# Two layers of a hybrid diffusion backbone on one core: the step of the bidirectional scan reordered, its first products and copies moved ahead of the attention branch

## What is computed

```python
proj = h @ w_in                      # q k v | z | xBC | dt | u gv | gates, 1024 x 6928
y_att = attend(q, k, v)
y_ssm = ssm_branch(z, xbc, dt, ...)  # bidirectional scan, 8 heads x 64, state 64
y_gm  = gmlp_branch(u, gv, ...)
merged = g0 * (y_att @ w_branch[0]) + g1 * (y_ssm @ w_branch[1]) + g2 * (y_gm @ w_branch[2])
return merged @ w_o, ...
```

```python
acs    = cumsum(dt * a)
decay  = exp(where(lower, acs[i] - acs[j], -inf))
scores = einsum('bcihn,bcjhn->bcijh', cc, bc) * decay          # C.B products times the decay
y_diag = einsum('bcijh,bcjhp->bcihp', scores, x * dt)
y_off  = einsum('bcihn,bchpn,bcih->bcihp', cc, h_in, exp(acs)) # C times exp(acs), times the initial state
y      = y_diag + y_off (+ the flipped direction) + x * d_skip
y      = rms_norm(y * silu(z), norm_g)
```

## Time and profile before

| | before |
|---|---|
| median of 3 runs | 1352.4 us |
| profiled execution, its own time | 1351.62 us |
| its span | 1349.8 us |
| mean granted TensorE clock | 0.960 |
| TensorE busy | 1252.7 us, 93% |
| weight loads of TensorE busy | 977.7 us, 72% |
| VectorE busy | 1006.4 us, 75% |
| ScalarE busy | 741.4 us, 55% |
| GpSimd busy | 67.1 us, 5% |
| moved by DMA | 353.68 MB, 262 GB/s |

### The profile page before, as it was taken

How to read it: one execution, slowest core, us unless ns; L and a number is a source line. 1 busy time by engine, 2 the same in 40 slices (tenths; PEclk the granted TensorE clock), 3 DMA queues, 4 the chain that set the end, 5 groups by cost and what they waited for, 6 DMA issues and landing times.

```text
span 1349.8 us, 16800 instructions
## 1 busy us (share of the span) xinstructions
PE 1252.7 (93%) x6097; PEld 977.7 (72%) x6097; DVE 1006.4 (75%) x1154; ACT 741.4 (55%) x704; POOL 67.1 (5%) x113
## 2 busy tenths in 40 slices
PE   5999999989899999999989999998987999999994
PEld 1767777777676787877767777786776768788773
DVE  0646557787688888888877466678857988888886
ACT  1543454652655667677653454356345666666773
POOL 1400001001000000000020000010000000000000
PEclk8899898999989999999989989998998999999998
DMA  9978654537778999899976767353435798989991
GB/s 357 306 276 313 232 182 148 180 118 302 264 255 311 338 329 342 317 341 340 354 224 211 265 253 258 130 187 133 165 139 200 287 352 325 328 318 338 348 355 60
DMA packets 98092, 353.68 MB, mean 262 GB/s; under 512 B 9060, under 2 KB 12608, under 8 KB 81616
## 3 DMA queue, kind: packets, MB, share of 16 engines
q1 hardware_dynamic: 87504, 295.12, 61.0%
q0 software_dynamic: 10496, 57.39, 12.1%
HBM read 349.77 MB, written 3.74 MB: 262 GB/s over the span
## 4 chain that ended last, share of the span: by engine, by line
PE 60%; DVE 24%; ACT 4%; DMA 4%; issue 3%; DVEq 3%; ACTq 1%; SPq 1%; POOL 0%; POOLq 0%
PE bank L910 57%; DVE wl L1785 13%; PE bank L913 3%; ACT wh L1684 1%; DMA first<-in_w_ada 1%; DVE tmp L1785 1%; ACT wh L1477 1%; DMA adaw<-in_w_ada 1%; DVE merged L1785 1%; DVE hid L2475 1%; DMA decay<-decay_rows 1%; DVE x L1785 1%; ACTq L1572 1%; DMA raw<-in_moe_w 1%; ACT gate L1571 0%
## 5 line engine op out<-in xcount | busy, mean ns | idle before, releaser
L1785 DVE TENSOR_TENSOR wl<-raw,wh 128x2048 fp32r<-128x2048 f32 (+1 forms) x268 | 610.5, 2278 | 125.8 <-ACT wh L1477 77.6
L1684 ACT ACTIVATE wh<-raw 128x2048 fp32r<-128x2048 f32 x192 | 367.5, 1917 | 61.9 <-PE bank L910 47.7
L910 PE MATMUL bank<-wh,xgh 128*128 128x512 f32 x512 | 212.2, 414 | 5.2 <-DVEq L2444 5.1
L910 PE MATMUL bank<-wh,xgl 128*128 128x512 f32 x512 | 204.9, 400 | 0.0
L910 PE MATMUL bank<-wl,xgh 128*128 128x512 f32 x512 | 204.5, 399 | 0.0
L1477 ACT ACTIVATE wh<-raw 128x2048 fp32r<-128x2048 f32 (+1 forms) x76 | 142.3, 1872 | 103.9 <-PE bank L910 62.1
L910 PE MATMUL bank<-wh,hTh 128*128 128x512 f32 x448 | 188.0, 420 | 5.6 <-DVE wl L1785 3.4
L910 PE MATMUL bank<-wl,hTh 128*128 128x512 f32 x448 | 183.1, 409 | 0.0
L910 PE MATMUL bank<-wh,hTl 128*128 128x512 f32 x448 | 182.5, 407 | 0.0
L910 PEld LDWEIGHTS bank<-wh,xgh 128*128 128x128 f32 x512 | 98.3, 192 | 25.3 <-DVE xgl L1785 5.4
L910 PEld LDWEIGHTS bank<-wh,xgl 128*128 128x128 f32 x512 | 97.7, 191 | 23.8
(11 more groups left out here) (302 smaller groups left out, 1556.9 us busy)
## 6 DMA issues: line engine op xcount, KB each, us to landing
raw<-in_moe_w SPq DMA_DIRECT2D x256, 512.0 KB, 4.9
raw<-in_moe_w SPq DMA_DIRECT2D x64, 1024.0 KB, 5.2
raw<-in_w_in SPq DMA_DIRECT2D x52, 1024.0 KB, 6.1
adaw<-in_w_ada POOLq DMA_DIRECT2D x32, 1024.0 KB, 7.0
raw<-in_w_branch SPq DMA_DIRECT2D x12, 1024.0 KB, 5.2
raw<-in_w_ada SPq DMA_DIRECT2D x8, 1024.0 KB, 9.8
raw<-in_w_o SPq DMA_DIRECT2D x8, 1024.0 KB, 4.7
first<-in_w_ada SPq DMA_DIRECT2D x4, 1024.0 KB, 16.7
```

The source lines that it names most:

```text
L910: return behind(nc.tensor.matmul(*args, **kw))
L1684: tally(A_(wh[c][:, :], raw[:, r, :], ACT.Copy), part_high[c])
L1785: return V.tensor_tensor(o, a, b, op)
```

## The change

Six things are done, in both layers:

1. On TensorE the products `cb00`, `cb01` go ahead of the last gate fill of branch 0, `xs0`, `cb10`, `cb11`, `xs1` behind it and ahead of the attention branch, `bt` behind that branch. Before, all of them stood behind the cumulative sums. The plan of the banks follows.
2. On ScalarE the two copies of `xs` stand between the last gate copy and the root of the gv norm.
3. On VectorE the copies `cb_of(0)`, `cb_of(1)` and the one to `btok` stand around the gv norm and the two conversions, ahead of `merge(0)`; before, behind `sumrow`.
4. `eb` holds only the rows that are used, for two steps: `[P, 2, 2, P]`. The exponential is two instructions of 64 partitions x 256 instead of one of 128 x 512. It waits for the reader of the step two before and not of the step before.
5. The two products to `ctS` move from behind the subtraction to the end of the step, behind the conversion, and the subtraction no longer waits for `eb`.
6. The product of x and the skip factor is a function of its own, `skipped`. For the context it runs in step 1 into the upper half of `tmp`, for the latent tokens ahead of `branch_turned(2)`.

```diff
@@ -207,13 +207,11 @@
     odd("adaT2")
     sides(4, 5, 6, 7)
     turned(0)
+    odd("cb00"), odd("cb01"), odd("xs0"), odd("cb10"), odd("cb11"), odd("xs1")
     branch(0)
+    odd("bt")
     odd("sp0"), odd("sp1")
     odd("ac"), odd("acT")
-    for s in range(2):
-        odd(f"cb{s}0"), odd(f"cb{s}1")
-        odd(f"xs{s}")
-    odd("bt")
     odd("st0"), odd("st1")
     for n in range(8):
         if n % 4 == 3:
@@ -445,7 +443,7 @@
             ("S", [P, 4, 2 * P], F32, 6),
             ("pT", [P, 2, 4, P], F32, 10),
             ("yTh", [P, BC, 2 * P], F32R, 0), ("yTl", [P, BC, 2 * P], F32R, 4),
-            ("W", [P, 2, 4, P], F32, 0), ("eb", [P, 4, P], F32, 4),
+            ("W", [P, 2, 4, P], F32, 0), ("eb", [P, 2, 2, P], F32, 4),
             ("ctS", [P, 2, 2, P], F32, 6),
             ("decay0", [P, 4, P], F32, 8),
             ("cbm", [P, 2, 2, P], F32, 10),
@@ -1158,8 +1156,30 @@
                 fill(("gate", 0, 1, 0))
                 turn_mod(l, 2, "adaT2")
                 branch_rows(l, 0, q)
+                pe.wait_ge(xbc_ready, 3 * l + 3)
+
+                def state_products(s):
+                    for g in range(2):
+                        t = bank_free(pe, l, f"cb{s}{g}")
+                        r = slice(g * HD, (g + 1) * HD)
+                        ins = mm(t[:, 0:P], xbc[r, 4, s * P:(s + 1) * P], xbc[r, 5, s * P:(s + 1) * P], start=True, stop=True)
+                        fills(ins, f"cb{s}{g}")
+
+                def turn_state(s):
+                    turn4(l, f"xs{s}", [xbc[:, m, s * P:(s + 1) * P] for m in range(4)])
+
+                state_products(0)
                 fill(("gate", 0, 1, 1))
+                turn_state(0)
+                state_products(1)
+                turn_state(1)
                 branch(l, 0)
+                t = bank_free(pe, l, "bt")
+                turn(t[:, 0:P], xbc[:, 4, 0:P], ident)
+                for g in range(2):
+                    ins = mm(t[g * HD:(g + 1) * HD, P:2 * P], ident[:, (1 - g) * HD:(2 - g) * HD], xbc[:, 5, P:2 * P],
+                             start=True, stop=True)
+                fills(ins, "bt")

@@ -1183,20 +1203,6 @@
-                pe.wait_ge(xbc_ready, 3 * l + 3)
...
                 fill(GATES[2][0])
                 pe.wait_ge(bt_ready, l + 1)
                 for r in range(2):
@@ -1628,6 +1634,8 @@
                 branch_turned(0)
                 ahead(("gate", 0, 1, 1))
                 gate_take(0, 1)
+                for s in range(2):
+                    take(f"xs{s}", xs[:, s, :], ACT.Copy, xs_ready)
                 square_root(0)
                 ahead(("branch", 0, 0))
                 ahead(("branch", 0, 1))
@@ -1635,8 +1643,6 @@
 
                 act.wait_ge(rem_ready, l + 1)
                 A_(acs[:, 0, 16:32], acs[:, 0, 16:32], ACT.Exp).then_inc(rem_exp, 1)
-                for s in range(2):
-                    take(f"xs{s}", xs[:, s, :], ACT.Copy, xs_ready)
                 ahead(GATES[2][0])
                 for r in range(2):
                     if r == 0:
@@ -1647,9 +1653,11 @@
                 for n in range(8):
                     if n >= 4:
                         act.wait_ge(decay_in[n % 2], 16 * (4 * l + n // 2 + 1))
-                        if n >= 5:
-                            act.wait_ge(ct_done, 4 * l + n - 4)
-                        A_(eb[:, :, :], decay[n % 2][:, :, :], ACT.Exp)
+                        if n >= 6:
+                            act.wait_ge(ct_done, 4 * l + n - 5)
+                        for r in range(2):
+                            gp = slice(r * HD, (r + 1) * HD)
+                            A_(eb[gp, n % 2], decay[n % 2][gp, r:4:2, :], ACT.Exp)
                         act.drain().then_inc(eb_exp, 1)
                     act.wait_ge(seg_in, 8 * l + n + 1)
                     A_(seg[:, n % 2], seg[:, n % 2], ACT.Exp)
@@ -2191,12 +2199,23 @@
                     filled(3 * i + 2)
                 ahead(("gate", 0, 1, 0))
                 modulation(l, 2, "adaT2")
+                cbraw = ropet[:, :].rearrange("p (s g t) -> p s g t", s=2, g=2)
+                def cb_of(s):
+                    for g in range(2):
+                        t = bank_full(dve, l, f"cb{s}{g}")
+                        frees(V.tensor_copy(cbraw[:, s, g, :], t[:, 0:P]), f"cb{s}{g}")
+
                 branch_turned(0)
+                cb_of(0)
                 ahead(("gate", 0, 1, 1))
                 gv_norm()
+                cb_of(1)
                 early = dve.mark_branch_hint_location()
                 ahead(("branch", 0, 0))
                 ahead(("branch", 0, 1))
+                t = bank_full(dve, l, "bt")
+                frees(V.tensor_copy(btok[:, :], t[:, 0:2 * P]), "bt")
+                drain().then_inc(bt_ready, 1)
                 merge(0)
 
 
@@ -2220,17 +2239,6 @@
                 frees(V.tensor_copy(sumrow[:, :], t[0:32, 0:2 * P]), "acT")
                 drain().then_inc(sums_rows, 1)
 
...
                 ahead(GATES[2][0])
 
                 dve.wait_ge(rem_exp, l + 1)
@@ -2241,22 +2249,23 @@
                     tt(xw[:, r, :].rearrange("t (h d) -> t h d", h=HEADS), xs[:, 0, :].rearrange("t (h d) -> t h d", h=HEADS),
                        bc(wend[:, 8 * r:8 * r + 8], 2, HD), ALU.mult)
                     drain().then_inc(xw_ready, 1)
-                def scanned(s):
+                def skipped(s, y):
+                    tt(y.rearrange("t (h d) -> t h d", h=HEADS), xs[:, s, :].rearrange("t (h d) -> t h d", h=HEADS),
+                       bc(hrow[:, 32:40], 2, HD), ALU.mult)
+                    drain()
+
+                def scanned(s, y, squares):
 
                     if s == 0:
                         dve.wait_ge(z_ready, 2 * l + 2)
-                    y = tmp[:, 0:NW]
-                    tt(y.rearrange("t (h d) -> t h d", h=HEADS), xs[:, s, :].rearrange("t (h d) -> t h d", h=HEADS),
-                       bc(hrow[:, 32:40], 2, HD), ALU.mult)
-                    drain()
                     t = bank_full(dve, l, f"y{s}")
                     frees(tt(y, t[:, :], y, ALU.add), f"y{s}")
                     drain()
                     tt(z[:, s, :], y, z[:, s, :], ALU.mult)
                     drain()
-                    tt(tmp[:, NW:D], z[:, s, :], z[:, s, :], ALU.mult)
-                    drain()
-                    V.tensor_reduce(small[:, s:s + 1], tmp[:, NW:D], X, ALU.add)
+                    tt(squares, z[:, s, :], z[:, s, :], ALU.mult)
+                    drain()
+                    V.tensor_reduce(small[:, s:s + 1], squares, X, ALU.add)
                     drain()
 
                 for n in range(9):
@@ -2265,21 +2274,12 @@
                         if n in (0, 1):
 
                             bank_full(dve, l, f"st{n}")
-                        if n >= 4:
-                            dve.wait_ge(eb_exp, 4 * l + n - 3)
                         dve.wait_ge(decay_in[n % 2], 16 * (4 * l + n // 2 + 1))
                         for i in range(4):
                             h, r = 2 * j + i // 2, i % 2
                             V.tensor_scalar(seg[:, n % 2, i, :], decay[n % 2][:, i, :],
                                                   acs[:, s, 8 * r + h:8 * r + h + 1], 0.0, ALU.subtract, ALU.min)
                         drain().then_inc(seg_in, 1)
-                        if n >= 4:
-                            dve.wait_ge(y_sem, 8 * l + n - 1)
-                            for r in range(2):
-                                gp = slice(r * HD, (r + 1) * HD)
-                                state_out = xbc[gp, 5, P:2 * P] if r == j // 2 else btok[gp, P:2 * P]
-                                ins = tt(ctS[gp, n % 2], eb[gp, r:4:2, :], bc(state_out, 1, 2), ALU.mult)
-                            ins.then_inc(ct_done, 1)
                     if n >= 1:
                         m = n - 1
                         s, j = m // 4, m % 4
@@ -2300,10 +2300,21 @@
                         drain().then_inc(W_ready, 1)
                     if 1 <= n < 8:
                         ahead(SCAN_FILL[n - 1])
+                    if 4 <= n < 8:
+                        dve.wait_ge(eb_exp, 4 * l + n - 3)
+                        dve.wait_ge(y_sem, 8 * l + n - 1)
+                        for r in range(2):
+                            gp = slice(r * HD, (r + 1) * HD)
+                            state_out = xbc[gp, 5, P:2 * P] if r == n % 4 // 2 else btok[gp, P:2 * P]
+                            ins = tt(ctS[gp, n % 2], eb[gp, n % 2], bc(state_out, 1, 2), ALU.mult)
+                        ins.then_inc(ct_done, 1)
+                    if n == 1:
+                        skipped(0, tmp[:, NW:D])
                     if n == 6:
-                        scanned(0)
+                        scanned(0, tmp[:, NW:D], tmp[:, 0:NW])
+                skipped(1, tmp[:, 0:NW])
                 branch_turned(2)
-                scanned(1)
+                scanned(1, tmp[:, 0:NW], tmp[:, NW:D])
```

27 lines of the change are left out of this document (2 added, 25 removed).

## The result

The changed kernel took 1354.65 us (median of 10 runs, 1350.47 to 1356.87), the kernel before beside it 1350.55 (median of 10, among them the three shown above). The ratio of the runs is 1.0026, 95% interval 1.0014 to 1.0038: under the 2% that counts as a change, but 3.5 us and clear of noise. The difference of the two medians is 4.1 us. I had forecast no difference. The profiled execution took 1355.28 us, its span is 1353.5 against 1349.8.

The account below looks back on a forecast made before the run. The chain ended last on TensorE for 60% of the span, but a VectorE-ScalarE loop bounded the changed stretch. Terms 2 x 0.1 + 2 x 0.0 + 0.5 - 0.7 gave 0.0 us, so 1352.4 us; range 1347.5 to 1358.

Parts of the forecast that it names:

- Front, ScalarE: Root of the gv norm: 0.45 us of passes and 1.4 of x copies ahead make it 1.85 late.
- Front, VectorE: Copies moved ahead of the row sums add 1.1 us; with the late root, their copy starts 2.95 later.
- the clock risk: Rival, chance 0.03: clock stays down after TensorE's 3.5 us wait before the states; some 2 us a layer, 1356.4.
- Front, TensorE: Next gate fill ends 5.3 us earlier; not kept, as state products wait 3.5 us for xw, running from 228.3.
- Start of the scan: First subtraction in layer 0: first decay tile lands last, at 230.65; scan starts at 230.7, 0.6 us earlier.
- an upper bound: Third step's start: +0.4 us if a 1 MB weight load competes with decay tiles or the clock falls.
- To sub 2: Third step's start, with the early skip product of 0.69 + 0.08: +0.1 us, between -0.6 and +0.4.
- Steps 4 to 7: Scan with ctS at step ends and eb's wait gone: -1.45, +0.5, +0.1, +0.87, together 0.0 us a layer.
- the slow rival: Chance 0.20: ctS at a step's end lengthens the loop over two engines, 2.7 us a layer, 1357.8.
- Tail: Second skip product ahead of the uT pair: nothing in layer 0, up to +0.77 in layer 1, taken as +0.5.
- layer 1's state bank: Layer 1's first subtraction had 0.7 us more to lose on the TensorE side, which the change takes: -0.7.

Follow-up runs that it names:

- the front alone: Kernel before with only the moved products, transposes and ScalarE's and VectorE's copies; scan, eb and skip products as before: ratio 1.0012 to the kernel before.
- with ctS back: Changed kernel with the two ctS products back between subtraction and W, eb still for two steps: one time of 1349.48 us.
- the load held back: Changed kernel with the SP queue holding one weight load until the first two decay tiles have landed: ratio 1.0025 to the kernel before.
- the scan part alone: Kernel before with only eb in halves for two steps, ctS at the end of a step and early skip products: ratio 1.0001 to the kernel before.

## Why the prediction was wrong

The forecast was a sum of terms that cancel, 0.0 us; measured are 3.5 us in the runs, and 4.0 in the two mixers.

- **Front, ScalarE.** Root 1.85 us late: 2.06 without the dip. Right. Not foreseen was that this path is not the only one. Without ScalarE's copies on it, the row sums are still 2.5 us late, because the copy to btok, moved ahead of the merge, then waits 1.18 us for TensorE. I counted the moved passes only as TensorE's own time, and looked for who waits for them only at the gate copy.
- **Front, VectorE.** Row sums 2.95 late: 2.93 in layer 1, in both layers of the front alone, and in both with ctS back. Right. In layer 0 of the profiled execution 1.55 more, from a clock dip at a place where I had none; I had placed the clock risk behind the new wait of TensorE.
- **Front, TensorE.** The fill was to end 5.3 us earlier and the state products to wait for xw. The trace of layer 0 shows a wait of 2.88 us for 3.5, full clock from 218.4 to 225.2 instead of 0.50, and state products at 229.13 for 230.08. Right in kind, and without value for the first subtraction, which a tile released.
- **Start of the scan: the step that failed.** "It lands at 230.65": I took 3.6 us for a tile from a row of a time in which no other transfer ran. It took 5.6 in layer 0 and 5.3 in layer 1, and 3.7 with the load held back. From the copy of the row sums to sub 0 it was 10.07 and 9.72 us instead of 8.05. I had named the meeting with the 1 MB load, but for the second tile and as an upper bound, with the load at 227.05 and the tiles at 227.0, and then took a point between the bounds. Both times were in my own working, so the meeting was no chance but a result, as all the other fronts confirm. With 5.6 us the scan starts at 232.7 instead of 230.7, 1.4 late instead of 0.6 early; the front alone, without a dip, has 1.41 in layer 0.
- **To sub 2.** I had +0.65 from sub 0 on for the skip product; it was +0.54 in layer 1, -0.06 in layer 0, and +0.28 and +0.38 in the scan part alone. In size that fits, but for another reason: the front by itself shortens this stretch by 0.48 and 0.64 us, and the skip product then adds its whole length.
- **Steps 4 to 7.** Forecast -1.45, +0.5, +0.1, +0.87, together 0.0. Measured in layer 0: 7.05 for 8.40 (-1.35), 7.66 for 7.05 (+0.6), 10.15 for 10.03 (+0.1), 8.26 for 7.39 to the last W (+0.87). Right, each of them, and the sum from sub 2 to the last W is +0.2. What the sum hid is that ctS in its new place costs 1.85 us a layer and the rest of the scan part gives 1.65 back; the slow rival had the mechanism and its place, and was wrong that the wait for eb would not pay for it.
- **Tail.** From the last W to the end 32.10 and 32.55 before, 32.11 and 32.56 after: nothing, also in layer 1, where I had +0.5. And -0.7 for layer 1's state bank: its first subtraction had waited 1.3 us longer for TensorE, and its mixer lost 2.06 us less than layer 0's. But 1.55 of these are the clock dip; in the front alone, with no dip, the layers are 1.5 apart. In sign that was right.

Added up: I had +0.1 us at sub 2 in layer 0, and -0.6 in layer 1 (0.1 less the 0.7), and it was +2.88 and +0.79. Of the 4.2 us between, 1.55 are the clock dip of layer 0, a term that I had put at nothing in this place, and 2.6 remain for the late landing, less what came back by sub 2. The scan steps added 0.35 where I had 0.0, and the tail's 0.5 did not come: 4.0 in all. So the largest error of the working was the price of one transfer, 2.0 and some 1.6 us at the first subtraction. That this price alone makes the 3.5 us of the runs is not shown: holding the load back made the tiles fast again and left the ratio at 1.0025, since the loads then met the next tiles. The range of 1347.5 to 1358 held the time.

## What to carry to other kernels

Price a transfer by what else is in flight when it is issued after the change, not by its row before: work out the time at which each neighbour starts, and if they meet, take the slow value and not a mean. A product that is moved for TensorE's sake has a second price: all that stands behind it on TensorE comes later, and so do the buffers it frees, and a reader that was moved up may now wait. And in a loop over two engines, work belongs ahead of the place where the one waits for the other: between subtraction and W two products of 0.42 us only shortened the wait for ScalarE's conversion, and behind that conversion they cost 1.85 us a layer over four steps. Last, two small moves can spoil each other: the skip product was to fill a wait that the new front had already removed.

## What was not expected of the hardware

- A 256 KB tile from POOL's queue landed in 3.5 to 3.8 us alone and in 5.3 to 6.4 when issued together with a 1 MB load of the SP queue, which took 6.7 to 7.1 instead of 4.9 to 5.0. In the scan part alone, layer 0, the load came 1.3 us after the first tile, which then took 4.2.
- The granted clock fell to 0.50 in 3 of 14 layers at the start of a fill behind an unbroken run of 20 or more narrow passes on TensorE, and did not in the two with twelve more of such passes. The cause is open.
- ScalarE's exponential in two halves of 64 partitions x 256 takes 0.84 us where one of 128 x 512 took 0.63: half the elements of a partition in each, but halving the width does not halve the time (a ScalarE activation of 128 x 256 takes 0.385).
